# A norm that scales after the turn, rows turned back beside the routing, and stationary router weights

## The reference

```python
h = rms_norm(x, norm_mix_g[layer]) * (1.0 + sc1) + sh1          # x: rows, h: input of the mixer
h2 = rms_norm(x, norm_ffn_g[layer]) * (1.0 + sc2) + sh2         # input of the experts
...
aff = jax.nn.sigmoid(jnp.dot(h2d, router_w).astype(F32))        # 16 experts in 4 groups
# best group by the sum of its two best, then the two best experts of that group
wts = wts / jnp.sum(wts, axis=-1, keepdims=True)
# rows are sorted by expert into blocks, each block goes through its expert
...
aff = jax.nn.softmax((h @ w_router).astype(jnp.float32), axis=-1)   # second block
top_aff, top_idx = lax.top_k(jnp.swapaxes(aff, 1, 2), cap)          # each expert picks 32 tokens
```

## Time and profile before

| | us |
|---|---|
| three runs | 3269.29, 3270.18, 3274.02; median 3270.18 |
| profiled execution | 3267.96 |
| its span | 3266.5 |
| PE busy, PEld busy | 2714.6, 1561.0 |
| DVE busy, ACT busy | 1285.1, 850.0 |
| POOL busy | 105.9 |
| mean granted clock of TensorE | 0.888 |
| HBM read | 780 MB, 250 GB/s over the span |

### The profile page before, as it was taken

One profiled execution on the slowest core, in us unless ns is written; L12 is line 12 of the kernel. 1 busy time (PEld: TensorE's weight loads), 2 busy tenths in 40 slices (PEclk: granted clock), 3 DMA queues, 4 the chain that ended last, 5 costly groups with the idle time before them and its releaser, 6 DMA issues.

```text
span 3266.5 us, 28213 instructions
## 1 busy us (share of the span) xinstructions
PE 2714.6 (83%) x11331; PEld 1561.0 (48%) x11331; DVE 1285.1 (39%) x2075; ACT 850.0 (26%) x1292; POOL 105.9 (3%) x172
## 2 busy tenths in 40 slices
PE   6988596959999996999777777769878996888787
PEld 3744474648888884556422222234455443222222
DVE  3377738459999995234310000032373013000001
ACT  2322323138788874022100000012112001000000
POOL 0011100010000001000000000000000000000000
PEclk8989898869999997965789999969989997999988
DMA  8399460159999995300379999962102332999997
GB/s 306 115 355 386 154 229 18 53 198 385 396 395 391 394 380 184 117 26 1 144 304 399 402 398 403 406 217 78 64 1 83 127 131 104 383 409 409 409 410 281
DMA packets 246925, 820.06 MB, mean 251 GB/s; under 512 B 11075, under 2 KB 11241, under 8 KB 246528
## 3 DMA queue, kind: packets, MB, share of 16 engines
q1 hardware_dynamic: 226688, 753.87, 59.9%
q0 software_dynamic: 14512, 46.28, 4.1%
q10 hardware_dynamic: 5584, 17.98, 1.4%
HBM read 780.20 MB, written 37.90 MB: 250 GB/s over the span
## 4 chain that ended last, share of the span: by engine, by line
PE 62%; DMA 23%; DVE 9%; issue 2%; ACT 2%; SPq 1%; POOL 1%; PEldq 0%; DVEq 0%; ACTq 0%; POOLq 0%
PE PS L245 59%; DMA ring<-in_moe_w_up 7%; DMA ring<-in_w_e_up 4%; DMA ring<-in_w_e_down 3%; DMA ring<-in_moe_w_gate 3%; DMA ring<-in_w_e_gate 2%; PE PS L2215 1%; PE PS L1674 1%; DMA ring<-in_moe_w_down 1%; SPq L374 1%; DMA ring<-in_ada_w 1%; DVE hgrn L898 0%; DVE SM L1316 0%; DMA row<-YP,DST 0%; DMA SM<-in_router_w 0%
## 5 line engine op out<-in xcount | busy, mean ns | idle before, releaser
L410 DVE TENSOR_TENSOR cut<-ring,cut 128x1024 fp32r<-128x1024 f32 x424 | 502.0, 1222 | 180.4 <-ACT cut L402 169.0
L402 ACT CAST cut<-ring 128x1024 fp32r<-128x1024 f32 x424 | 437.2, 1051 | 266.3 <-PE PS L245 240.3
L245 PE MATMUL PS<-cut,xeT 128*128 128x512 f32 x1536 | 364.6, 394 | 3.2 <-DVE cut L410 3.2
L245 PEld LDWEIGHTS PS<-cut,xeT 128*128 128x128 f32 x1536 | 285.9, 189 | 67.4 <-DVE cut L410 6.4
L245 PE MATMUL PS<-ring,hidT 128*64 128x512 f32 (+1 forms) x1024 | 249.5, 639 | 66.1 <-DMA ring<-in_w_e_down 27.2
L245 PE MATMUL PS<-ring,xeT 128*64 128x512 f32 x1024 | 242.8, 623 | 65.6 <-DMA ring<-in_moe_w_up 33.2
L245 PE MATMUL PS<-ring,XE 128*32 128x512 f32 x1008 | 249.4, 649 | 53.3 <-DMA ring<-in_w_e_up 33.7
L245 PE MATMUL PS<-HT,ring 128*128 128x512 f32 (+2 forms) x576 | 206.8, 526 | 0.7 <-DVE HT L506 0.7
L245 PEld LDWEIGHTS PS<-ring,xeT 128*64 128x64 f32 x1024 | 77.9, 142 | 229.0 <-issue 170.6
L245 PE MATMUL PS<-cut,hidT 128*128 128x512 f32 x768 | 179.7, 394 | 4.5 <-DVE hidT L1683 4.5
L245 PEld LDWEIGHTS PS<-ring,hidT 128*64 128x64 f32 (+1 forms) x1024 | 71.7, 131 | 230.6 <-issue 174.4
(11 more groups left out here) (517 smaller groups left out, 2876.2 us busy)
## 6 DMA issues: line engine op xcount, KB each, us to landing
ring<-in_moe_w_gate SPq DMA_DIRECT2D x64, 2048.0 KB, 13.0
ring<-in_moe_w_up SPq DMA_DIRECT2D x64, 2048.0 KB, 12.2
ring<-in_moe_w_down SPq DMA_DIRECT2D x64, 2048.0 KB, 12.6
ring<-in_w_e_up SPq DMA_DIRECT2D x32, 2048.0 KB, 18.4
ring<-in_w_e_down SPq DMA_DIRECT2D x32, 2048.0 KB, 19.3
ring<-in_w_e_gate SPq DMA_DIRECT2D x31, 2048.0 KB, 18.4
ring<-in_ada_w SPq DMA_DIRECT2D x24, 2048.0 KB, 13.6
ring<-in_w_in SPq DMA_DIRECT2D x13, 2048.0 KB, 7.6
```

The source lines that it names most:

```text
L245: return pe.matmul(o, l, r, start=start, stop=stop, **kw)
L402: act.copy(self.bufs[i % len(self.bufs)][0], w).then_inc(self.high.sem, 1)
L410: dve.tensor_tensor(low, w, high.bitcast(F32), ALU.subtract).then_inc(self.low.sem, 1)
```

## The change

- `normed`: nothing is spread. `MOD` itself is turned, eight 12x128 tiles into bank 7, and DVE copies it to `MT` (features on partitions, one column per modulation row), ahead of the reciprocal. DVE multiplies the even chunks and ACT the odd ones by their reciprocals alone, which gives `U`. PE turns the tiles of `U`, two features' tiles of a pair of chunks to a bank; the copies out to `HT`, 256 columns each and two to a bank, multiply by the scale column and add the shift column (ACT the odd banks, DVE the even ones).
- Where rows are needed (both routings and the last experts), PE turns `HT` back, four tiles to a bank, and ACT copies the banks to `H`; POOL's scatters and the gathering matmuls wait for these copies.
- Routers: the weights, padded with zeros from 16 to 32 columns (a POOL memset, waited for, ahead of the load), are the stationary operand and `HT` the moving one, eight matmuls in four strips of 32 rows; DVE copies these partial sums, and one matmul per chunk with a constant adds the four strips up and turns them. The constant `C_SUM` grows to 16 columns for that.
- Routing: `M` is made before the weights are summed; the counts come from one triangular matmul and one with ones per chunk over all later chunks at once; `ew` is made before the logits.

The core of the diff (semaphores, their retirement and the widths of small tiles are left out):

```diff
-        c[32 * q:32 * q + 12, C_SUM:C_SUM + 12] = np.eye(12)
+        c[32 * q:32 * q + 16, C_SUM:C_SUM + 16] = np.eye(16)
...
-    def normed(chunks, shift, scale, H, HT, rs, squares, there=()):
+    def normed(chunks, shift, scale, U, HT, rs, squares, there=()):
 
 
         n = len(chunks)
         groups = [r for r in range(2) if any(c // 2 == r for c in chunks)]
+        nb = 4 * len(groups)
+        MT = chunked(column(1880, 96), 8)
...
+        def of_bank(t):
+
+            r = groups[t // 4]
+            for j in range(2):
+                k = 2 * (t % 4) + j
+                yield (HT[:, k, 256 * r:256 * r + 256], bank(t)[:, 256 * j:256 * j + 256],
+                       MT[:, k, scale + r:scale + r + 1], MT[:, k, shift + r:shift + r + 1])
...
-                for t in range(1, 2 * n, 2):
-                    i, g = divmod(t, 2)
+                act.wait_ge(*inverted(0))
+                for i in range(1, n, 2):
+                    act.mul(U[:, chunks[i], :], X[:, chunks[i], :], rs[:, i:i + 1]).then_inc(odd_made.sem, 1)
+                act.wait_ge(*mod_kept(0))
+                for t in range(1, nb, 2):
                     act.wait_ge(*turned(t))
-                    act.copy(HT[:, 4 * g:4 * g + 4, chunks[i] * P:(chunks[i] + 1) * P],
-                             chunked(bank(t), 4)).then_inc(odd.sem, 1)
+                    for dst, src, by, plus in of_bank(t):
+                        ins = act.activation(dst, src, ACT.Identity, bias=plus, scale=by)
+                    ins.then_inc(odd.sem, 1)
...
+                dve.wait_ge(*mod_turned(0))
+                dve.tensor_copy(MT, chunked(bank(7)[:, 0:96], 8)).then_inc(mod_kept.sem, 1)
                 dve.wait_ge(*rooted(0))
-                vs.add(dve.reciprocal(rs[:, 0:n], rs[:, 0:n]))
-                dve.wait_ge(*vs.now)
-                for i, c in enumerate(chunks):
-                    r = groups.index(c // 2)
-                    dve.wait_ge(*spread(2 * r))
-                    vs.add(dve.scalar_tensor_tensor(out=H[:, c, :], in0=X[:, c, :], scalar=rs[:, i:i + 1],
-                                                    in1=bank(4 * r, 2), op0=ALU.mult, op1=ALU.mult))
-                    dve.wait_ge(*vs.now)
-                    dve.wait_ge(*spread(2 * r + 1))
-                    dve.tensor_tensor(H[:, c, :], H[:, c, :], bank(4 * r + 2, 2), ALU.add).then_inc(made.sem, 1)
-                for t in range(0, 2 * n, 2):
-                    i, g = divmod(t, 2)
+                dve.reciprocal(rs[:, 0:n], rs[:, 0:n]).then_inc(inverted.sem, 1)
+                dve.wait_ge(*inverted(0))
+                for i in range(0, n, 2):
+                    dve.tensor_scalar(U[:, chunks[i], :], X[:, chunks[i], :], rs[:, i:i + 1], None, ALU.mult).then_inc(even_made.sem, 1)
+                dve.wait_ge(*mod_kept(0))
+                for t in range(0, nb, 2):
                     dve.wait_ge(*turned(t))
-                    dve.tensor_copy(HT[:, 4 * g:4 * g + 4, chunks[i] * P:(chunks[i] + 1) * P],
-                                    chunked(bank(t), 4)).then_inc(even.sem, 1)
+                    for dst, src, by, plus in of_bank(t):
+                        ins = dve.tensor_scalar(dst, src, by, plus, ALU.mult, ALU.add)
+                    ins.then_inc(even.sem, 1)
...
-                for r, of in enumerate(groups):
-                    for w, row in enumerate((scale + of, shift + of)):
-                        for h in range(2):
-                            last = mm(bank(4 * r + 2 * w + h), ident[0:12, row:row + 1].to_broadcast([12, P]),
-                                      MOD[:, h * 512:h * 512 + 512], True, True)
-                        last.then_inc(spread.sem, 1)
-                for t in range(2 * n):
-                    i, g = divmod(t, 2)
-                    pe.wait_ge(*made(i | 1))
-                    for k in range(4):
-                        last = pe.transpose(bank(t)[:, k * P:(k + 1) * P],
-                                            H[:, chunks[i], (4 * g + k) * P:(4 * g + k + 1) * P], ident)
+                for k in range(8):
+                    last = pe.transpose(bank(7)[:, 12 * k:12 * k + 12], MOD[:, k * P:(k + 1) * P], ident[0:12, 0:12])
+                last.then_inc(mod_turned.sem, 1)
+                for t in range(nb):
+                    r = groups[t // 4]
+                    if t % 4 == 0:
+                        pe.wait_ge(*even_made(t // 4))
+                        pe.wait_ge(*odd_made(t // 4))
+                    if t == nb - 1:
+                        pe.wait_ge(*mod_kept(0))
+                    for j in range(2):
+                        k = 2 * (t % 4) + j
+                        for c in range(2):
+                            last = pe.transpose(bank(t)[:, 256 * j + c * P:256 * j + (c + 1) * P],
+                                                U[:, 2 * r + c, k * P:(k + 1) * P], ident)
...
+            pool.memset(rw, 0.0).then_inc(rw_set.sem, 1)
+            pool.wait_ge(*rw_set(0))
+            pool.dma_start(rw3[:, :, 0:16], I["router_w"].rearrange("(c p) e -> p c e", p=P)).then_inc(rw_in.sem, 16)
             pool.dma_start(rb, to_all(I["router_b"], 16)).then_inc(rb_in.sem, 16)
             pool.wait_ge(*placed_(0))
-            pool.wait_ge(*norm.rows(nch - 1))
+            pool.wait_ge(*row_made(2 * nch - 1))
...
-                    last = mm(bank(0)[:, i * 16:i * 16 + 16], HT[:, k, c * P:(c + 1) * P], rw3[:, k, :], k == 0, k == 7)
+            for k in range(8):
+                q = k % 4
+                last = mm(bank(0)[32 * q:32 * q + 32, 0:nch * P], rw3[:, k, :], HT[:, k, 0:nch * P], k < 4, k > 3, skip_group_check=True)
+            last.then_inc(parts_made.sem, 1)
+            for t in range(2 * nch):
+                c, g = divmod(t, 2)
+                if t == 4:
+                    route_sums()
+                if t > 5:
+                    pe.wait_ge(*row_made(t - 6))
+                for j in range(4):
+                    last = pe.transpose(bank(2 + t % 6)[:, j * P:(j + 1) * P], HT[:, 4 * g + j, c * P:(c + 1) * P], ident)
+                last.then_inc(row_turned.sem, 1)
+            if nch == 2:
+                route_sums()
+            pe.wait_ge(*chosen(0))
+            b = bank(1)[:, 128:128 + N + 16]
+            mm(b, KC[:, C_LT:C_LT + P], M, True, False)
+            for j in range(1, nch + 1):
+                last = mm(b[:, 16 * j:N + 16], ones, M[:, 0:N + 16 - 16 * j], False, j == nch)
+            last.then_inc(counted.sem, 1)
+
+        def route_sums():
+
+            pe.wait_ge(*parts_kept(0))
+            for i in range(nch):
+                last = mm(bank(1)[:, i * 16:i * 16 + 16], parts[:, i * P:(i + 1) * P], KC[:, C_SUM:C_SUM + 16], True, True)
             last.then_inc(logits.sem, 1)
-            pe.wait_ge(*chosen(0))
-            b = bank(1)
-            for i in range(nch):
-                for j in range(i):
-                    mm(b[:, i * 16:i * 16 + 16], ones, M[:, j * 16:j * 16 + 16], j == 0, False)
-                mm(b[:, i * 16:i * 16 + 16], KC[:, C_LT:C_LT + P], M[:, i * 16:i * 16 + 16], i == 0, True)
-            for j in range(nch):
-                last = mm(b[:, 64:80], ones, M[:, j * 16:j * 16 + 16], j == 0, j == nch - 1)
-            last.then_inc(counted.sem, 1)
 
         def route_scalar():
+            def rows(ts):
+                for t in ts:
+                    c, g = divmod(t, 2)
+                    act.wait_ge(*row_turned(t))
+                    act.copy(H[:, c, 512 * g:512 * g + 512], bank(2 + t % 6)).then_inc(row_made.sem, 1)
+
             act.wait_ge(*logits(0))
-            act.activation(aff, bank(0)[:, 0:N], ACT.Sigmoid).then_inc(chance.sem, 1)
+            act.activation(aff, bank(1)[:, 0:N], ACT.Sigmoid).then_inc(chance.sem, 1)
+            rows(range(2 * nch))
...
+            for s in norm.ready:
+                dve.wait_ge(*s)
+            dve.wait_ge(*parts_made(0))
+            dve.tensor_copy(parts, bank(0)[:, 0:nch * P]).then_inc(parts_kept.sem, 1)
+            dve.memset(M[:, N:N + 16], 0.0)
+            vs.settle(dve.tensor_scalar(ew, KC[:, C_EX:C_EX + 16], -1.0, 16.0, ALU.mult, ALU.add))
...
+            dve.tensor_tensor(M[:, 0:N], o1, o2, ALU.add).then_inc(chosen.sem, 1)
             for k, o in enumerate((o1, o2)):
                 vs.settle(dve.tensor_tensor(t2, o, aff, ALU.mult))
                 vs.settle(dve.tensor_reduce(wk[k], v3(t2), AX.X, ALU.add))
@@ -1548,10 +1595,9 @@
             vs.settle(dve.reciprocal(den, den))
             for k in range(2):
                 vs.settle(dve.tensor_tensor(wk[k], wk[k], den, ALU.mult))
-            dve.tensor_tensor(M, o1, o2, ALU.add).then_inc(chosen.sem, 1)
             dve.wait_ge(*counted(0))
-            vs.settle(dve.tensor_copy(pos, bank(1)[:, 0:N]))
-            vs.settle(dve.tensor_copy(cnt, bank(1)[:, 64:80]))
+            vs.settle(dve.tensor_copy(pos, bank(1)[:, 128:128 + N]))
+            vs.settle(dve.tensor_copy(cnt, bank(1)[:, 128 + N:144 + N]))
...
```

(19 more changed lines are left out.)

64 lines of the change are left out of this document (36 added, 28 removed).

## The result

| | before | after |
|---|---|---|
| median, us | 3269.73 (3268.94 to 3274.02, 4 executions) | 3212.68 (3209.91 to 3220.7, 4 executions) |
| profiled execution, its span | 3267.96, 3266.5 | 3211.93, 3210.4 |
| PE, PEld busy | 2714.6, 1561.0 | 2635.0, 1529.9 |
| DVE, ACT busy | 1285.1, 850.0 | 1253.5, 877.7 |
| mean granted clock | 0.888 | 0.900 |

The ratio is 0.9827 (95% interval 0.9807 to 0.9846): 57 us faster. The forecast was 3215 us, the range 3206 to 3230.

The account below looks back on a forecast made before the run. No single bound: long stretches bound by DMA or DVE's cutting, with short serial stretches between, where all edits lie. 41.2 + 5.1 + 0.2 + 0.7 + 5.8 + 2.6 = 55.6 us gave 3212.4 profiled, 3215 us median; range 3206 to 3230.

Parts of the forecast that it names:

- The norms: All six norms: -41.2 us together; with four chunks, 8.3 us from the reciprocal's end to the last copy.
- the sign: What would show the prediction right: reciprocal to last copy takes 8 to 9 us in the four norms of four chunks.
- Layer 1's routing wins nothing from its norm: Layer 1's routing: the logits already wait for the router's weights, so an earlier norm gains nothing; +0.3 us with the memset.
- The routers: Logits with stationary weights: -5.1 us in layer 0 (6.0 for 11.09), -0.2 in layer 1, -0.7 in the last.
- The counting: Routings, early M, fewer counting instructions and earlier ew: -5.8 us in layer 0, -2.6 us in layer 1.
- Rows turned back: Routings and last block: ACT's copies lie beside DVE's routing and cost nothing; without that cover 2 to 5 us.
- The last norm: Two chunks before the last router: weights land 7.1 us after issue, logits start at 2732.0 instead of 2739.25, -7.2 us.
- Half clock in all turns: Rival: turns hold PE's clock down in four norms and two routers, +11.2 us, 3226 us; chance 0.12.
- The router late in the last norm too: Rival: router weights take 11.2 us in the last norm, +4.1, and layer 1 another 4.1; 3223 us, chance 0.10.
- Projection and attention: Two rivals: layer 1's projection at half clock, 3312 us, chance 0.03; window attention at full clock, 3155 us, chance 0.03.
- Gains lost further on: Rival: an unseen load ends the stretch and up to half the gain is lost, 3227 to 3243 us; chance 0.06.

Follow-up runs that it names:

- e1_old_logits: The changed kernel with the logits of both routings made the old way, normalised activations stationary; 3219.75 us, ratio 0.984.
- e2_old_count: The changed kernel with M made after the chances' weights and the old 14 and 5 counting products; 3219.91 us, ratio 0.9846.
- e3_router_first: The changed kernel with layer 1's router weights issued ahead of six other loads on GpSimd's queue; 3208.44 us, ratio 0.9803.
- e11_states_filled: The changed kernel with filler products before the second block's state-sum steps and six after the last; 3198.56 us, ratio 0.9768.
- e6_warm_products: The changed kernel with extra products with the identity on PE ahead of the six norms' own turns; 3212.92 us, ratio 0.9815.
- e9_all_three: The changed kernel with layer 0's router kept and the last loaded earlier, extra turns before the norms, and state-sum fillers; 3182.43 us, ratio 0.9719.

## Why the prediction was right

- **The norms** (41.2 us forecast). Undoing them cost 38 to 42 us. The steps held one by one: the reciprocal to the last copy takes 7.95 us in layer 0 (forecast 8.3), 7.7 in layer 1 and in the second block (the sign said 8 to 9 us in all four), 8.77 in the first norm. In that one PE came out of a pause of 6.70 us and ran longer at half clock, 6.39 us for the 32 turns in place of 5.65. A scaled copy of 256 columns takes 0.54 us on DVE and 0.56 on ACT (forecast 0.56, bounds 0.37 and 0.78), two in a row 0.99 and 1.02. The row scaling on DVE, 0.71 to 0.86 us a chunk, was above the 0.62 forecast, under the cover of ACT's 1.15.
- **Layer 1's routing wins nothing from its norm**: held to 0.15 us (15.24 against 15.1 us).
- **The routers.** Layer 0: 11.09 us became 4.66, -6.4 in place of -5.1. I took 6.0 us, 0.9 above the sum at full clock, 5.1; it came in under that sum too, as the three groups of PE overlap a little (they start 1.85 and 1.81 us apart) and the hand-over took 0.04 us. (The upper bound of that term adds up to 9.5 us, not 9.4.) Undone alone the same part gives 4.95 us to the scatter and 5.65 to the sigmoid (10.31 from the first old product): behind the new norm the old products run faster too, 10.28 us in place of 11.09. Layer 1: the mis-sized term is the turns back, priced at 3.7 us of half clock; they took 2.71, because the clock rises among them, and the sums 0.52 in place of 0.9. It measured -2.07, not -0.2. In three of the other profiles the turns took the 3.68 us priced, and the gain would be 0.8 to 1.1 us: part of this is luck of the clock.
- **The counting**: 5.8 and 2.6 us forecast, 5.58 and 2.48 measured.
- **Rows turned back, "cost nothing"**: right for ACT's copies, wrong by 0.7 and 1.3 us for PE's turns ahead of the sums. The routers' terms had these turns in them (in the 6.0 and the 6.8 us), so the sum wasn't hurt, but their price had been called none.
- **The last norm**: the weights landed 8.1 us after their issue (forecast 7.1), and PE stood 1.2 us longer for them than for the norm. The landing varies, though: in e1_old_logits, e2_old_count and e3_router_first, with that load as it was, it took 6.8 to 7.2 us, and 41.5 us passed to the first expert, 0.8 less.
- **What was missed**: 5.5 us of clock in the state sums. It was hidden by 3.9 us more than forecast in the stretches with an edit and 2.8 us in those without. The forecast of 3212.4 for the profiled execution against 3211.93 is thus better than its working, and that is luck. The state sums and layer 1's stretch behind the attention each move by 4 to 6 us between profiles, without an edit to them; the prediction had no such term, and gave the measurement's own uncertainty as 6.5 us.
- **The rivals.** Half clock in all turns: no, 5.2 to 6.4 us. The router late in the last norm too: by 1 us, not 4. Projection and attention: clock as before. (The price of the slow projection was inconsistent: a third of its 97 us at half clock costs 32 us; to eat the gain of 55 us more than half of it would have to run so.) Gains lost further on: 6 us, in a place that no rival named.

## What to carry to other kernels

Price every instruction that stands in the queue ahead of a short critical one, even if "other engines" cover it: the sixteen turns before the tiny sums were the only part of the work called free that cost anything, 0.7 and 1.3 us. Before a short stage is rebuilt, look at what its inputs' loads wait behind: one reordering of GpSimd's issues gave 7 us where a faster norm gave none. And where an engine pauses for some microseconds before each short burst, throwaway work of the same kind in the pause can pay, here 17 us for 37 products. Leave little of the pause: where 3.9 us of it were left, nothing was gained. And run the unedited kernel's profile more than once before reading an effect of 5 us from one: two stretches that nobody touched moved by that much.

## What the runs showed of the hardware

- Turns by TensorE bring its clock up: 28 extra ones, and the next 32 take 3.69 us in place of 6.39 (granted clock 1.00 in place of 0.57).
- Eight instructions of 384 columns take 5.46 us at 1.2 GHz and 2.82 at 2.4 GHz. Behind pauses of 3.7 to 5.9 us most of the steps start at the low clock; but behind one of 3.87 us the same step took 5.46 us in both profiles of the changed kernel and 2.82 us in that of the kernel before. In e11_states_filled, with at most 1.3 us of pause left, five of six took 2.85 us and the first 3.36.
- A load of 64 KB in small pieces (the router) lands after 3.1 or 5.0 us in layer 0, after 9.8 to 11.8 us behind a context transfer in layer 1 (10.6 in the kernel after), and after 6.5 us ahead of it.
- One kernel's executions lie up to 11.6 us apart (five of e3_router_first) or as little as 1.9 us (four of e6_warm_products). Filling the pauses of the state sums doesn't decide that: 4.9 us in e9_all_three, 8.0 in e11_states_filled.
